# Computing layer 1's modulation vectors piece by piece during layer 0's expert stage

## The chip, the cores and the metric

The kernel runs on one core of a Trainium2 chip. The metric is the device time of one execution in microseconds (us); the time given for a kernel is the median of its runs. The core has TensorE (PE, with its weight loads PEld), VectorE (DVE), ScalarE (ACT), GpSimd (POOL), SyncE (SP), which here only issues transfers, and 16 DMA engines.

## What is computed

Two blocks, one after the other, on 256 tokens of 1024 features, each with two layers. Only the first block is touched by the change. Its layer, cut to what matters here:

```python
cond = jax.nn.silu(c)                       # c: (1, 1024)
for l in range(DEPTH):                      # DEPTH = 2
    mod = cond @ ada_w[l] + ada_b[l]        # 1024 x 6144: the modulation
    sh1, sc1, g1, sh2, sc2, g2 = split(mod, 6)
    h = rms_norm(x, norm1_g[l]) * (1.0 + sc1) + sh1
    proj = h @ w_in[l]                      # then three mixers on its parts
    x = x + g1 * (concat(y_ssd, y_moba, y_swa) @ w_out[l])
    h = rms_norm(x, norm2_g[l]) * (1.0 + sc2) + sh2
    x = x + g2 * peer_ffn(h, ...)           # 8 heads x top 16 of 16384 experts
```

The modulation depends on c alone, not on x: that of layer 1 can be computed at any time. The expert stage peer_ffn is done densely: all 16384 experts' pre-activations are computed (first layer, u), multiplied with a gate that is zero for experts not chosen, and multiplied with v (second layer).

## The kernel before

Products are in fp32 split into two halves of type fp32r ("upper" and "lower"). Each weight part of 1 MB (128x2048 f32) is loaded by SyncE into one of four slots raw, ScalarE copies its upper half (upper_part, L1164), and VectorE (L1494) or GpSimd (L622) subtracts to get the lower half (lower_part). TensorE makes three passes: upper by lower, upper by upper, lower by upper (by_feature L685 and L691, by token L715 and L722, second_layer L920). A slot of raw is free for part n once the lower half of part n - 4 is made; ScalarE and VectorE prepare part n + 2 in turn n (SPLIT = 2).

**The modulation** is the first thing of a layer: twelve tiles of 1024x512 (2 MB, in_ada_w). VectorE sums chunks 0 to 5 of a tile by scalar_tensor_tensor (L1555, L1558), TensorE does chunks 6 and 7 (L760), the bias (L765), and sums VectorE's part over the partitions with a matrix of ones (L767); ScalarE writes the result, the same in all partitions, to mod (L1147). The tiles' slots are the memory in which the weight parts also lie, so in layer 1 the loads start when layer 0's last parts are used up. Between tiles 3 and 4 VectorE norms x and, in both layers, the memory tokens mem, whose transposed form goes out to DRAM.

**The expert stage** of a layer has 128 turns n, in the order of expert_order(): 40 first_layer parts, then two first_layer and two second_layer parts in alternation to turn 87, then 40 second_layer parts. Turns 0 to 19 lie beside the choice of the experts on VectorE; GpSimd makes their lower halves. Turns 20 to 35 also build the gates: for each group of 8 tokens VectorE makes one-hot matrices (hot(i), L1824 and L1825, 16 instructions), TensorE multiplies them (gate_group, L899), ScalarE copies the result to gates_out (L1274), and SyncE writes each pair of groups to DRAM (spill, L565), 1 MB. From there fetch (L574) brings them back by experts. In a loop turn VectorE does, in this order, gate_hidden (where there is one), lower_part(n + 2), and hot for the two groups of the next turn. hot(i) waits for group i - 2. The four zero matmuls that open the accumulators acc (L891) stand before turn 20.

**SyncE's list** in the expert stage is what sets the order of the transfers:

```python
for n, (layer, t, u) in enumerate(expert_order()):
    e = expert_part(l, 0, n)
    sp.wait_ge(*e.raw_free())
    sp.dma_start(raw[:, e.r, :], ...)
    if 0 <= n - 2 * CHOOSE - RAW < GROUPS // 2:      # n = 24 to 39
        spill(n - 2 * CHOOSE - RAW)                  # waits for groups up to 2 (n - 24) + 1
```

Each engine runs a list of its own, in order; a wait holds back all that stands behind it. The first block's two layers are the two turns of a loop (Fori) on each engine.

## Time and profile before

| | us |
|---|---|
| median of 3 runs | 3761.12 |
| lowest and highest | 3759.5, 3761.81 |
| the profiled execution | 3763.92 |
| its span | 3762.1 |
| PE busy | 3430.5 (91%) |
| DVE busy | 2390.1 (64%) |
| ACT busy | 1468.7 (39%) |
| mean DMA | 183 GB/s |

Layer 0 of the first block takes the span from 0 to 1101 us, layer 1 from there to 2193 us, the second block the rest. The busy times are those of the whole span; the stages differ much, so they are read one by one. Busy PE is not PE at its peak. L12 is line 12 of the kernel before.

### The profile page before, as it was taken

The numbers are of one execution on the slowest core, as the hardware profiler recorded it, in microseconds if no ns is written. First come the engines' busy times: TensorE is split into PE (matmuls) and PEld (weight loads), VectorE is DVE, ScalarE is ACT, GpSimd is POOL, SyncE is SP. The second block draws the span as 40 slices with busy tenths as digits, with TensorE's granted clock in tenths as the row PEclk, the third lists the DMA queues.
The fourth block names the chain that finished last, engine by engine and source line by source line (L and its number), as shares of the span: only waits on it lengthen the run. The fifth ranks groups of instructions, "written<-read, shape, count | busy, mean of one in ns | idle before, by whom it ended". The sixth has DMA issues, their size and how long they took to land.

```text
span 3762.1 us, 58692 instructions
## 1 busy us (share of the span) xinstructions
PE 3430.5 (91%) x22220; PEld 3103.9 (83%) x22220; DVE 2390.1 (64%) x4104; ACT 1468.7 (39%) x1545; POOL 229.0 (6%) x48
## 2 busy tenths in 40 slices
PE   6879999999988799999999989996999898968898
PEld 2879899998864789899998889785889797957896
DVE  6657996556777759995557765464545454644454
ACT  1434454333322434444333343443443433434433
POOL 0005600000000008200000000000000000000000
PEclk8989999999998899999999999998999999979999
DMA  8424466667766234466666755450444454513453
GB/s 361 168 77 158 157 224 242 212 210 235 240 254 271 95 126 176 180 233 232 209 215 236 242 215 179 163 195 23 157 148 168 163 180 157 194 53 127 144 180 123
DMA packets 154051, 688.78 MB, mean 183 GB/s; under 512 B 10338, under 2 KB 76770, under 8 KB 78946
## 3 DMA queue, kind: packets, MB, share of 16 engines
q1 hardware_dynamic: 149264, 663.79, 49.6%
q10 hardware_dynamic: 4564, 22.21, 1.6%
q8 instruction: 116, 1.90, 0.2%
q14 instruction: 107, 0.88, 0.1%
HBM read 649.26 MB, written 36.70 MB: 182 GB/s over the span
## 4 chain that ended last, share of the span: by engine, by line
PE 79%; DVE 11%; ACT 3%; issue 2%; DVEq 2%; DMA 1%; PEld 1%; ACTq 0%; PEldq 0%
PE ps L685 25%; PE ps L920 19%; PE ps L691 12%; PE ps L715 9%; PE ps L722 4%; PE ps L899 3%; DMA work<-in_mem 1%; ACT work L1156 1%; PE ps L760 1%; DVE position_hot L1801 1%; PE ps L657 1%; DVE position_hot L1804 1%; DVE scr L1759 1%; DVE scr L1766 1%; PE ps L767 1%
## 5 line engine op out<-in xcount | busy, mean ns | idle before, releaser
L1164 ACT ACTIVATE weights_upper<-weights 128x2048 fp32r<-128x2048 f32 x520 | 995.8, 1916 | 1747.4 <-PE ps L685 972.4
L1494 DVE TENSOR_TENSOR weights_lower<-weights,weights_upper 128x2048 fp32r<-128x2048 f32 x476 | 1089.4, 2289 | 789.9 <-ACT weights_upper L1164 789.1
L685 PE MATMUL ps<-hT_upper,weights_upper 128*128 128x256 f32 x4416 | 626.2, 284 | 3.0 <-ACT hT_upper L1326 2.7
L685 PE MATMUL ps<-hT_lower,weights_upper 128*128 128x256 f32 x4416 | 624.9, 284 | 0.2
L691 PE MATMUL ps<-hT_upper,weights_lower 128*128 128x256 f32 x4416 | 575.3, 283 | 4.2 <-POOL weights_lower L622 4.2
L685 PEld LDWEIGHTS ps<-hT_upper,weights_upper 128*128 128x128 f32 x4416 | 572.0, 192 | 6.4 <-ACT hT_upper L1326 6.3
L685 PEld LDWEIGHTS ps<-hT_lower,weights_upper 128*128 128x128 f32 x4416 | 571.3, 192 | 4.7 <-issue 1.0
L691 PEld LDWEIGHTS ps<-hT_upper,weights_lower 128*128 128x128 f32 x4416 | 549.7, 192 | 5.0 <-POOL weights_lower L622 5.0
L622 POOL TENSOR_TENSOR weights_lower<-weights,weights_upper 128x2048 fp32r<-128x2048 f32 x44 | 228.8, 5213 | 1300.6 <-ACT weights_upper L1164 1300.6
L920 PE MATMUL ps<-weights_upper,hidden_lower 128*128 128x512 f32 x1024 | 253.6, 390 | 0.0
L920 PE MATMUL ps<-weights_lower,hidden_upper 128*128 128x512 f32 x1024 | 252.9, 389 | 0.0
L920 PE MATMUL ps<-weights_upper,hidden_upper 128*128 128x512 f32 x1024 | 252.9, 389 | 0.0
L920 PEld LDWEIGHTS ps<-weights_upper,hidden_upper 128*128 128x128 f32 x1024 | 192.2, 188 | 39.9
L920 PEld LDWEIGHTS ps<-weights_lower,hidden_upper 128*128 128x128 f32 x1024 | 192.2, 188 | 39.9
L920 PEld LDWEIGHTS ps<-weights_upper,hidden_lower 128*128 128x128 f32 x1024 | 190.7, 188 | 38.6
L1825 DVE TENSOR_SCALAR scr<-cst,scr 128x128 f32<-128x128 f32 x512 | 177.2, 346 | 0.0
L1824 DVE TENSOR_SCALAR scr<-cst,scr 128x128 f32<-128x128 f32 x512 | 149.8, 292 | 0.2
L1841 DVE TENSOR_TENSOR hidden_upper<-work,scr 128x512 fp32r<-128x512 f32 x80 | 55.4, 692 | 119.3 <-PE ps L920 119.3
L899 PE MATMUL ps<-scr 128*128 128x128 f32 x1024 | 121.4, 277 | 0.0
L899 PEld LDWEIGHTS ps<-scr 128*128 128x128 f32 x1024 | 119.1, 191 | 0.0
L715 PE MATMUL ps<-weights_upper,ffn_lower 128*128 128x512 f32 x352 | 101.0, 407 | 18.3 <-DVE ffn_lower L1974 18.3
L657 PE MATMUL ps<-diag,x_res 128*128 128x128 f32 x256 | 49.6, 382 | 72.7 <-DVE diag L1905 72.7
(311 smaller groups left out, 3496.6 us busy)
## 6 DMA issues: line engine op xcount, KB each, us to landing
weights<-in_parts SPq DMA_DIRECT2D x264, 1024.0 KB, 4.8
weights<-in_experts SPq DMA_DIRECT2D x256, 1024.0 KB, 4.8
weights<-in_ada_w SPq DMA_DIRECT2D x24, 2048.0 KB, 10.9
scr<-gates SPq DMA_DIRECT2D x32, 1024.0 KB, 8.2
gates<-h SPq DMA_DIRECT2D x16, 1024.0 KB, 4.8
gates<-work SPq DMA_DIRECT2D x16, 1024.0 KB, 4.8
mod<-in_row ACTq DMA_DIRECT2D x3, 1536.0 KB, 6.4
rowp<-in_row ACTq DMA_DIRECT2D x2, 1550.0 KB, 19.7
```

The lines of the kernel that those rows point to most:

```text
L622: g.tensor_tensor(lower[:, p_.r % SPLIT, :], raw[:, p_.r, :], upper[:, p_.r % SPLIT, :].bitcast(F32), ALU.subtract).then_inc(lower_ready, 1)
L657: m = mm(k.bank(name, i)[:, (2 * e + t) * P:(2 * e + t + 1) * P], x[:, t, c * P:(c + 1) * P], diag[:, t, :], start=True, stop=True, skip_g ...
L685: m = mm(bank[:, e * T:(e + 1) * T], up[:, c, e * P:(e + 1) * P], s_[:, c, :], start=(e == 0 and n == 0 and c == 0), stop=False, skip_grou ...
L691: m = mm(bank[:, e * T:(e + 1) * T], lo[:, c, e * P:(e + 1) * P], src[0][:, c, :], start=False, stop=(c == KC - 1), skip_group_check=True)
L715: m = mm(k.bank(name, fill + t)[:, 0:cols], s_[:, c, t * P:(t + 1) * P], up[:, c - 4 * i, 0:cols], start=(n == 0 and c == 0), stop=False, ...
L722: m = mm(k.bank(name, fill + t)[:, 0:cols], src[0][:, c, t * P:(t + 1) * P], lo[:, c - 4 * i, 0:cols], start=False, stop=(c == chunks - 1) ...
L899: m = mm(k.bank("G", j)[:, t * P:(t + 1) * P], hotA[:, i_buf, 4 * j + t, :], hotB[:, i_buf, 4 * j + t, :], start=True, stop=True, skip_gro ...
L920: m = mm(k.bank("acc", 2 * t_ + dh), src[:, u, c, t_ * P:(t_ + 1) * P], w[:, c, dh * NBLK:(dh + 1) * NBLK], start=False, stop=False, skip_ ...
L1164: f(upper[:, p_.r % SPLIT, :], raw[:, p_.r, :], ACT.Copy).then_inc(upper_ready, 1)
L1494: v.tensor_tensor(lower[:, s, :], raw[:, p_.r, :], upper[:, s, :].bitcast(F32), ALU.subtract)\
L1824: v.tensor_scalar(hotA[:, i % 2, j, :], iota, ET[:, 0, t:t + 1], None, ALU.is_equal)
L1825: m = v.tensor_scalar(hotB[:, i % 2, j, :], iota, ET[:, 1, t:t + 1], ET[:, 2, t:t + 1], ALU.is_equal, ALU.mult)
```

## The change

Layer 0's modulation stays as it is. That of layer 1 is computed on VectorE in 24 tiles of 256 columns, each of four pieces (256 rows each, 256 KB): ada_piece(s) adds two chunks of 128 rows, weighted by cond, to an accumulator ada_acc that starts from the bias row. Pieces 0 to 31 are done two a turn in turns 20 to 35, pieces 32 to 95 one a turn in turns 40 to 103 (ada_sub_step). SyncE loads a piece five turns (from turn 40 three turns) further on in its list (load_ada). TensorE sums a finished tile over the partitions with one column of ones, into one row (ada_rows, two turns after the last piece), ScalarE copies the row (ada_take), SyncE writes it to DRAM (keep_row), and ScalarE fetches it back, broadcast to all partitions, into mod (mod_back), in three loads near and after layer 0's end. Layer 1 then starts with a norm like that of h2 (scaled_and_shifted), from sums of squares made by ScalarE. mem is normed and kept in layer 0 only. The loads of the parameters of layer 1 move into layer 0's turns. The zero matmuls for acc now stand behind turn 39. The loops over the first block's layers, and those inside TensorE's expert stage, are written out. The host lays out ada_w[1] in the pieces' order.

```diff
@@ -37,6 +37,10 @@
 GROUPS = T // 8
 CHOOSE = 10
 AHEAD = CHOOSE + GROUPS // 4 + 2
+ADA_COLS = 256
+ADA_TILES = 6 * D // ADA_COLS
+ADA_SUBS = 4 * ADA_TILES
+LACED = GROUPS // 2
 EXPERTS = 4 * TURNS
 EPS1, EPS2 = 1e-5, 1e-6
 
@@ -45,6 +49,7 @@
...
@@ -204,6 +218,12 @@
     return order
 
 
+def ada_sub_step(s):
+
+
+    return 2 * CHOOSE + s // 2 if s < 2 * LACED else 2 * AHEAD + s - 2 * LACED
+
+
 class At:
...
@@ -453,6 +476,14 @@
         hotA = view(scr, 768, 2048, "p (b t i) -> p b t i", b=2, t=8)
         hotB = view(scr, 2816, 2048, "p (b t i) -> p b t i", b=2, t=8)
         gates_out = [view(b, at_, 2048, "p (i t) -> p i t", t=16) for b, at_ in ((h_all, 0), (work, 14336))]
+        ada_acc = [view(scr, 4864 + 256 * j, 256) for j in range(2)]
+        ada_bias_row = view(scr, 5376, 256)
+        ada_row = [scr[0:1, 5632 + 256 * j:5888 + 256 * j] for j in range(2)]
+
+        def ada_sub(s):
+
+            return view(work, (12288 if s < 2 * LACED else 14336) + 512 * (s % 4), 512, "p (c n) -> p c n", c=2)
+
         gates_in = view(scr, 768, 4096, "p (b g i t) -> p b g i t", b=2, g=16, i=8)
...
@@ -575,11 +606,32 @@
                                  gates_dram[:, :, 8 * n:8 * n + 8, :].rearrange("g p i t -> p g (i t)"))\
                         .then_inc(gates_landed[n % 2], 16)
 
+                def load_ada(s):
+
+                    tile = s // 4
+                    if s == 0:
+                        sp.wait_ge(S("chosen"), 1)
+                        sp.wait_ge(S("bias_zero"), 1)
+                        sp.sem_inc(S("held"), 1)
+                    if s % 4 == 0:
+                        if tile:
+                            sp.wait_ge(S("ada_used"), s - 3)
+                        sp.dma_start(ada_bias_row[0:1, :], a["ada_b"][1:2, tile * ADA_COLS:(tile + 1) * ADA_COLS])\
+                            .then_inc(S("ada_bias_in"), 16)
+                    if s >= 4:
+                        sp.wait_ge(S("ada_used"), s - 3)
+                    sp.dma_start(ada_sub(s).rearrange("p c n -> p (c n)"), a["ada_s"][s]).then_inc(ada_landed[s % 4], 16)
+
+                def keep_row(tile):
+
+                    sp.wait_ge(S("ada_taken"), tile + 1)
+                    sp.dma_start(ada_dram[0:1, tile * ADA_COLS:(tile + 1) * ADA_COLS], ada_row[tile % 2])\
+                        .then_inc(ada_kept[tile % 2], 16)
+
                 for n, (layer, t, u) in enumerate(expert_order()):
                     e = expert_part(l, 0, n)
                     sp.wait_ge(*e.raw_free())
-                    sp.dma_start(raw[:, e.r, :], a["experts"][bass.ds(l, 1), n].rearrange("o p n -> p (o n)"))\
-                        .then_inc(raw_landed[e.r], 16)
+                    sp.dma_start(raw[:, e.r, :], a["experts"][l, n]).then_inc(raw_landed[e.r], 16)
                     if 0 <= n - 2 * CHOOSE - RAW < GROUPS // 2:
                         spill(n - 2 * CHOOSE - RAW)
                     if n == 2 * CHOOSE + RAW + GROUPS // 2 + 1:
@@ -587,11 +639,18 @@
                         fetch(1)
                     if layer == 1 and u == 1 and t % 2 == 1 and 2 <= (t + 1) // 2 < TURNS // 2:
                         fetch((t + 1) // 2)
+                    if l + 1 < DEPTH:
+                        for s in range(ADA_SUBS):
+                            if ada_sub_step(s) + (5 if s < 2 * LACED else 3) == n:
+                                load_ada(s)
+                        for tile in range(ADA_TILES):
+                            if ada_sub_step(4 * tile + 3) + 10 == n:
+                                keep_row(tile)
...
-                    by_feature(expert_part(l, it, n), k.bank("U", u), hT1)
-
-                with pe.Fori(0, CHOOSE // 2) as it:
-                    for n in range(4):
-                        first_layer(it, n, it * 2 + n // 2, n % 2)
+                    by_feature(expert_part(l, 0, n), k.bank("U", u), hT1)
+
+                def ada_rows(n):
+
+                    for tile in range(ADA_TILES if l + 1 < DEPTH else 0):
+                        if ada_sub_step(4 * tile + 3) + 2 == n:
+                            name, i = ("early row", tile) if tile < LACED // 2 else ("late row", tile - LACED // 2)
+                            pe.wait_ge(*k.free(name, 0, i))
+                            pe.wait_ge(S("ada_used"), 4 * tile + 4)
+                            mm(k.bank(name)[0:1, 0:ADA_COLS], ones[:, 0:1], ada_acc[tile % 2], start=True, stop=True,
+                               skip_group_check=True).then_inc(k.fill_sem(name), 1)
+
+                order = expert_order()
+                for n in range(2 * CHOOSE):
+                    first_layer(n, *order[n][1:])
 
                 pe.wait_ge(S("chosen"), l + 1)
                 for i in range(2):
...
@@ -886,9 +956,6 @@
                         m = nc.tensor.transpose(k.bank("eT", i)[:, j * P:(j + 1) * P],
                                                 E3[:, 2 * i + j // 2, (j % 2) * P:(j % 2 + 1) * P], ident)
                     m.then_inc(k.fill_sem("eT", i), 1)
-                for i in range(4):
-                    pe.wait_ge(*k.free("acc", i))
...
@@ -896,21 +963,23 @@
                     for j in range(2):
                         pe.wait_ge(*k.free("G", j, i))
                         for t in range(4):
-                            m = mm(k.bank("G", j)[:, t * P:(t + 1) * P], hotA[:, i_buf, 4 * j + t, :],
-                                   hotB[:, i_buf, 4 * j + t, :], start=True, stop=True, skip_group_check=True)
+                            m = mm(k.bank("G", j)[:, t * P:(t + 1) * P], hotA[:, i % 2, 4 * j + t, :],
+                                   hotB[:, i % 2, 4 * j + t, :], start=True, stop=True, skip_group_check=True)
                         m.then_inc(k.fill_sem("G", j), 1)
 
-                with pe.Fori(0, GROUPS // 8) as it:
-                    for n in range(4):
-                        first_layer(it, 2 * CHOOSE + n, it * 2 + (CHOOSE + n // 2), n % 2)
-                        for i_buf in range(2):
-                            gate_group(it * 8 + (2 * n + i_buf))
-                for n in range(2 * CHOOSE + GROUPS // 2, 2 * AHEAD):
-                    first_layer(0, n, n // 2, n % 2)
-
-                def second_layer(it, n, t, u):
-
-                    p_ = expert_part(l, it, n)
+                for n in range(2 * CHOOSE, 2 * AHEAD):
+                    first_layer(n, *order[n][1:])
+                    if n < 2 * CHOOSE + LACED:
+                        for i in range(2):
+                            gate_group(2 * (n - 2 * CHOOSE) + i)
+                    ada_rows(n)
+                for i in range(4):
+                    pe.wait_ge(*k.free("acc", i))
+                    mm(k.bank("acc", i), zeros, cst[:, 0:NBLK], start=True, stop=False, skip_group_check=True)
...
@@ -1275,9 +1362,36 @@
                           k.bank("G", j).rearrange("p (t i) -> p i t", t=4), ACT.Copy)\
                             .then_inc(k.empty_sem("G", j), 1)
 
+                def ada_take(tile):
+
+                    name, i = ("early row", tile) if tile < LACED // 2 else ("late row", tile - LACED // 2)
+                    if tile >= 2:
+                        act.wait_ge(ada_kept[tile % 2], 16 * (tile // 2))
+                    act.wait_ge(*k.filled(name, 0, i))
+                    act.sem_inc(S("held"), 1)
+                    f(ada_row[tile % 2], k.bank(name)[0:1, 0:ADA_COLS], ACT.Copy).then_inc(k.empty_sem(name), 1)
+                    act.wait_ge(*k.emptied(name, 0, i))
+                    act.sem_inc(S("ada_taken"), 1)
+
                 for n, (layer, t, u) in enumerate(expert_order()):
                     if n + SPLIT < EXPERTS:
                         upper_part(expert_part(l, 0, n + SPLIT))
+                    elif l + 1 < DEPTH:
+                        upper_part(part(firsts[l + 1], 0, "win", n + SPLIT - EXPERTS))
+                    if l + 1 < DEPTH:
+                        if n == 2 * CHOOSE + LACED:
+                            act.wait_ge(S("ada_used"), 2 * LACED)
+                        for tile in range(ADA_TILES):
+                            if ada_sub_step(4 * tile + 3) + 3 == n:
+                                ada_take(tile)
+                        if n == 2 * AHEAD + 4 * (TURNS - AHEAD):
+                            mod_back(0, 2)
+                        if n == 112:
+                            act.wait_ge(S("gated"), 2 * (AHEAD + 3))
+                            mod_back(2, 5)
+                        if n == 118:
+                            act.wait_ge(S("gated"), 2 * (AHEAD + 6))
+                            row1_in(1)
                     if layer == 0:
                         gelu(n, t, u)
                     if n == 2 * CHOOSE - 5:
@@ -1288,11 +1402,21 @@
                             gates(2 * (n - 2 * CHOOSE) + i)
                     if n == 2 * AHEAD:
                         act.wait_ge(S("chosen"), l + 1)
-                        act.dma_start(final_g, a["final_g"].rearrange("(o n) -> o n", o=1).broadcast_to([P, D]))\
-                            .then_inc(S("fin_in"), 16)
-                        act.dma_start(colp[:, 0:K2["end"]], a["col2"][0]).then_inc(S("col_in"), 16)
-                act.wait_ge(S("fin_in"), l * 16 + 16)
-                act.wait_ge(S("col_in"), l * 16 + 16)
+                        if l + 1 < DEPTH:
+                            col1_in(1)
+                        else:
+                            act.dma_start(final_g, a["final_g"].rearrange("(o n) -> o n", o=1).broadcast_to([P, D]))\
+                                .then_inc(S("fin_in"), 16)
+                            act.dma_start(colp[:, 0:K2["end"]], a["col2"][0]).then_inc(S("col_in"), 16)
+                if l + 1 < DEPTH:
+                    for t in range(TT):
+                        act.wait_ge(S("x_peer"), l * TT + (t + 1))
+                        square_sum(x[:, t, :], h[:, t, :], t)
+                        deviation(t, t, EPS1_COL)
+                    act.wait_ge(S("first_done"), l + 2)
+                    mod_back(5, 6)
+            act.wait_ge(S("fin_in"), 16)
+            act.wait_ge(S("col_in"), 16)
 
             def rows(l, name, n, signal):
...
+                        v.scalar_tensor_tensor(out=h[:, t, :], in0=x[:, t, :], scalar=RS[:, t:t + 1], in1=gain,
+                                               op0=ALU.mult, op1=ALU.mult)
+                        v.drain()
+                        v.tensor_tensor(h[:, t, :], h[:, t, :], shift, ALU.add).then_inc(S(signal), 1)
+
+                if l == 0:
+                    for i in range(12):
+                        v.wait_ge(*k.emptied("ada", i))
+                    modulated(0, "h1")
+                    for i in (0, 2):
+                        take(k, "mT", i, mem_t[:, 2 * i:2 * i + 2, :])
+                    for n in range(2):
...
@@ -1844,8 +1977,29 @@
                     v.tensor_tensor(hid_lo[:, u, :, :], gact[t % AHEAD][:, u, :, :], hid_up[:, u, :, :].bitcast(F32),
                                     ALU.subtract).then_inc(S("gated"), 1)
 
+                def ada_piece(s):
+
+                    tile = s // 4
+                    acc = ada_acc[tile % 2]
+                    if s % 4 == 0:
+                        if tile >= 2:
+                            j = tile - 2
+                            v.wait_ge(*(k.filled("early row", 0, j) if j < LACED // 2
+                                        else k.filled("late row", 0, j - LACED // 2)))
+                        v.wait_ge(S("ada_bias_in"), 16 * tile + 16)
+                        v.sem_inc(S("held"), 1)
+                    v.wait_ge(ada_landed[s % 4], 16 * (s // 4) + 16)
+                    for c in range(2):
+                        v.drain()
+                        i = 2 * (s % 4) + c
+                        m = v.scalar_tensor_tensor(out=acc, in0=ada_sub(s)[:, c, :], scalar=cT[:, i:i + 1],
+                                                   in1=acc if i else ada_bias_row, op0=ALU.mult, op1=ALU.add)
+                    m.then_inc(S("ada_used"), 1)
+
                 hot(0)
                 hot(1)
+                if l + 1 < DEPTH:
+                    v.memset(ada_bias_row, 0.0).then_inc(S("bias_zero"), 1)
                 v.wait_ge(*expert_part(l, 0, 2 * CHOOSE + SPLIT - 1).lower())
                 for n, (layer, t, u) in enumerate(expert_order()):
                     if n < 2 * CHOOSE:
@@ -1855,13 +2009,27 @@
                         gate_hidden(t + 1, u)
                     if n + SPLIT < EXPERTS:
                         lower_part(expert_part(l, 0, n + SPLIT))
+                    elif l + 1 < DEPTH:
+                        lower_part(part(firsts[l + 1], 0, "win", n + SPLIT - EXPERTS))
                     i = 2 * (n - 2 * CHOOSE) + 2
                     if i < GROUPS:
                         hot(i)
                         hot(i + 1)
+                    if l + 1 < DEPTH:
+                        for s in range(ADA_SUBS):
+                            if ada_sub_step(s) == n:
+                                ada_piece(s)
+                        if n == 122:
+                            v.wait_ge(S("mod_in"), 32)
+                            v.wait_ge(S("par1_in"), 64)
+                            v.sem_inc(S("held"), 1)
+                            v.scalar_tensor_tensor(out=mod[:, D:2 * D], in0=mod[:, D:2 * D], scalar=1.0,
+                                                   in1=rowp[:, R1["n1"]:R1["n1"] + D], op0=ALU.add, op1=ALU.mult)
                     if n == 2 * AHEAD - 3:
                         gate_hidden(0, 0)
                         gate_hidden(0, 1)
+                if l:
+                    v.wait_ge(S("mod_in"), 48)
                 for t in range(TT):
                     for nb in range(2):
...
@@ -1874,9 +2042,9 @@
                 v.drain().then_inc(S("first_done"), 1)
 
 
-            v.wait_ge(S("fin_in"), 16 * DEPTH)
+            v.wait_ge(S("fin_in"), 16)
```

## Rows read from the trace of the kernel before

**Rows 1.** Busy time by stage: window, length, busy us (count) of PE PEld DVE ACT POOL, clock, DMA.
```profile
441.10:596.90 155.80, 155.80 (x1331) 155.80 (x1330) 147.67 (x512) 78.61 (x97) 0.00 (x0) 1.00 0.59 212
596.90:872.40 275.50, 275.50 (x1826) 254.66 (x1825) 157.82 (x121) 107.91 (x77) 0.00 (x0) 1.00 0.65 221
1100.90:1193.60 92.70, 63.36 (x139) 23.35 (x138) 75.23 (x105) 16.88 (x25) 0.00 (x0) 0.83 0.83 338
```

**Rows 2.** Timeline of one turn: start us, us, engine, line, operation.
```profile
512.35 3.79 PE L899 MATMUL ps<-scr 128*128 128x128 f32 x32
...
513.29 2.30 DVE L1494 TENSOR_TENSOR weights_lower<-weights,weights_upper 128x2048 fp32r<-128x2048 f32 x1
...
515.50 0.29 DVE L1824 TENSOR_SCALAR scr<-cst,scr 128x128 f32<-128x128 f32 x1
...
516.19 0.60 ACT L1274 ACTIVATE work<-ps 128x512 f32<-128x512 f32 x1 [0.30 <-PE ps L899]
...
516.87 0.33 SPq L565 DMA_DIRECT2D gates<-work  x1
...
517.49 0.33 SPq L581 DMA_DIRECT2D weights<-in_experts  x1
...
522.74 2.29 DVE L1494 TENSOR_TENSOR weights_lower<-weights,weights_upper 128x2048 fp32r<-128x2048 f32 x1
```

**Rows 3.** Timeline of the stage's first two turns.
```profile
447.05 2.29 DVE L1494 TENSOR_TENSOR weights_lower<-weights,weights_upper 128x2048 fp32r<-128x2048 f32 x1 [2.35 <-ACT weights_upper L1164]
...
456.51 2.28 DVE L1494 TENSOR_TENSOR weights_lower<-weights,weights_upper 128x2048 fp32r<-128x2048 f32 x1
...
460.59 0.33 SPq L565 DMA_DIRECT2D gates<-work  x1
```

**Rows 4.** Waits of SyncE's queue: in total us, times, longest.
```profile
SPq L564 <- ACT h L1274: 147.9, 16, 17.6
```

**Rows 5.** Timelines of three hand-overs: behind the experts, before h2T, before yT.
```profile
1101.02 1.29 DVE L1869 TENSOR_TENSOR scr<-ps,mod 128x512 f32<-128x512 f32 x2 [6.73 <-PE ps L941]
...
1199.68 0.87 PEld L715 LDWEIGHTS ps<-weights_upper,hT_upper 128*128 128x128 f32 x4
...
1312.37 3.27 PEld L641 LDWEIGHTS ps<-cst,h 128*128 128x128 f32 x16 [10.31 <-issue]
...
1321.58 0.87 PEld L715 LDWEIGHTS ps<-weights_upper,hT_upper 128*128 128x128 f32 x4
...
1341.99 0.16 DVE L1735 RECIPROCAL stats<-stats 128x1 f32<-128x1 f32 x1 [0.99 <-ACT stats L1142]
...
1346.32 1.23 DVE L1740 TENSOR_TENSOR h<-h,mod 128x1024 f32<-128x1024 f32 x1
...
2193.29 1.29 DVE L1869 TENSOR_TENSOR scr<-ps,mod 128x512 f32<-128x512 f32 x2 [6.73 <-PE ps L941]
...
2198.45 0.29 ACT L1142 ACTIVATE stats<-stats 128x1 f32<-128x1 f32 x1
```

**Rows 6.** One line's instructions: durations ns min/median/max, first and last start, forms.
```profile
L1712 DVE SCALAR_TENSOR_TENSOR h<-h,stats,rowp x12: 479/480/752, 216.8 to 1311.6; 128x256 f32<-128x256 f32 x8, 128x512 f32<-128x512 f32 x4
```

**Rows 7.** Groups by line, 1100.9 to 1194: busy, mean ns, idle time before.
```profile
L1558 DVE SCALAR_TENSOR_TENSOR mod<-weights,stats,mod 128x512 f32<-128x512 f32 x60 | 45.1, 751 | 4.5
```

**Rows 8.** Chain of work, in layer 1's modulation: start us, us, what.
```profile
1119.51 3.34 PE ps L760 x4
...
1125.21 1.95 PE ps L760 x4
```

**Rows 9.** DMA issues between 430 and 600 us: KB each, us to landing.
```profile
weights<-in_experts SPq DMA_DIRECT2D x18, 1024.0 KB, 6.7
gates<-h SPq DMA_DIRECT2D x8, 1024.0 KB, 4.8
```

**Rows 10.** Landing of the loads of line 1293 (colp, 164 KB).
```profile
DMA to landing us min/median/max: 3.6/3.9/4.1
```

**Rows 11.** Timeline of a turn with second_layer alone.
```profile
1090.02 0.69 DVE L1841 TENSOR_TENSOR hidden_upper<-work,scr 128x512 fp32r<-128x512 f32 x1 [1.09 <-PE ps L920]
```

238 lines of the change are left out of this document (129 added, 109 removed).

## The prediction

> **What bounds the kernel now.** I read the table of busy time by stages first, because the change touches one stretch of layer 0 and the stretch behind it. In layer 0's gate stage (441 to 597 us) and behind it TensorE is busy all the time at the full clock; between 1101 and 1194 us, where layer 1's modulation is computed, it is busy 63 of 93 us, VectorE 75, and the DMA engines 83% [rows 1]. So a transfer and a sum of 93 us lie bare between two expert-bound stretches, and what is worth asking is what the 16 turns before them can carry. A "turn" is one n of expert_order(); turns 20 to 35 of layer 0 each hold one first_layer part and two gate groups.
>
> The second view is the timeline of one such turn [rows 2]. TensorE's two gate groups take 3.8 us of it, the expert part the rest. VectorE repeats after 9.45 us (522.74 - 513.29): lower_part 2.2 us, then two hot() of 3.63 us each (7.26 us, from 515.50 to the next lower_part). It has no idle time in between, so the stage runs on two engines at once: whatever is added to VectorE here is added to the span. Over the whole stage VectorE waits once, 2.35 us before its first lower_part [rows 3].
>
> The third view is SyncE, which issues the transfers in program order. Its spill of a pair of gate groups waits for ScalarE's last copy of these groups; where that copy went to h, 16 such waits make 147.9 us [rows 4], and there are as many for the copies that go to work. In turn 21 the spill goes out at 460.59, while VectorE was done with the hot() of these groups before 456.51 [rows 3]. SyncE is thus paced by the gate groups, one spill per turn.
>
> **What the change removes, step by step.** From the first DVE instruction behind the expert sum (L1869, 1101.02) to the second win part (1199.68) before: 98.7 us [rows 5]. After: x of the first token tile, Square, table load and Sqrt take 5.45 us (2193.29 to 2198.45 + 0.29, the same chain before the final norm); from there two reciprocals, scalings and additions of 128x1024 take 5.56 us (1341.99 to 1346.32 + 1.23) and 0.1 of hand-over; then the second half of 16 transposes, upper and lower halves and the first part of a by-token product take 7.6 us (1314.0, the middle of the transposes that start at 1312.37, to 1321.58) [rows 5]. Sum 18.8 us, so 79.9 us are removed. Layer 1's twelve loads of 2 MB, their matmuls, the second norm of mem and its write all go with it; SyncE, ScalarE and VectorE have two win parts ready before, since these ride in the last two turns. ScalarE's Exp for a_log with its table load comes while VectorE makes h1, and is hidden.
>
> **What it adds in turns 20 to 35.** Each turn gets two pieces (ada_piece), each two scalar_tensor_tensor of 128x256 with a drain. One of 128x256 takes 0.48 us, one of 128x512 0.75 [rows 6]; a drain puts 0.07 between two of them (4.5 us of idle time for 60) [rows 7]. Four make 2.2 us, with the waits 2.3.
>
> The larger term is when their data comes. load_ada(s) stands in SyncE's list at n = turn + 5, behind spill(n - 24) of the same n, that is spill(turn - 19). This spill needs gate group 2(turn - 19) + 1 copied out; TensorE makes that group in turn + 1, from the hot() that VectorE does last in this same turn, right before it waits for the piece. So VectorE asks for data whose load is issued only after its own last result has gone through TensorE, ScalarE, the spill and the queue. The wait can't be worked off in advance; it comes in every turn. Its length from the end of hot():
> - TensorE's group: 1.9 us at full speed (half of 3.79), start and hand-over 0.1; ScalarE's last copy 0.6 and 0.1 of hand-over, so the spill goes out 2.7 us after hot() (from rows 2: matmuls end 516.14, copy 516.19 to 516.79, spill 516.87). TensorE will have stood idle some 8 us before it. Behind the pauses of the modulation stretch its matmuls ran at 1.2 GHz: 3.34 us for four against 1.95 at 2.4 GHz [rows 8]; the first of the two groups would take about 3.7 us and part of the second too. All of the last group slow would be 4.6 us, none 2.7; I take 3.7, half of it slow, since in rows 8 the full clock was back 5.7 us after a slow stretch had begun, which is about where the last group is half done.
> - the landing: a spill of 1 MB lands after 4.8 us. An expert part of 1 MB issued 0.6 us behind a spill lands after 6.7, not 4.8 [rows 9]. With S for the spill's issue that is S + 7.3, which is the spill's 4.8 and 2.5 for its own 1 MB. A piece is a quarter of that, so the first lands at S + 5.4, the second at S + 6.1. Issue (0.62 apart [rows 2]) is in time for that. Were small loads to pass the spill, the nearest row is colp's load, behind one of final_g, which lands after 3.6 to 4.1 [rows 10]: S + 0.6 + 3.6 = S + 4.2 at the least.
> - the two pieces, 2.3 us, the second of which has landed by then.
>
> So 3.7 + 5.4 + 2.3 = 11.4 us a turn. The last hot() is in turn 34, so 14 turns (20 to 33) delay it: 160 us. Ends: 2.7 + 4.2 + 2.3 = 9.2, or 129 us; 4.6 + 5.4 + 2.3 and 1.1 more if each 128x256 took what 128x512 took (0.75), 13.4, or 188 us.
>
> The Trainium skill, "TensorE: Matmul & The Clock Gate", section "HAM oscillation — how this bites in real kernels", says that a loop whose matmul bursts are separated by waits for DMA starts every burst at the low clock again. The trace agrees for a single pause (3.34 against 1.95 us); that it recurs each turn nothing in it shows. By the rule the last group is late by 1.0 us a turn, without it the sum would be 14 us lower. The skill's "DMA: Bandwidth & Descriptors", section "Anatomy of one DMA — SWDGE (gpsimd) path", puts the fixed cost of a transfer at about 2 us; a piece that met no queue would land about 2.6 us after its issue, an estimate by that page, and the sum would be 14 x 2.2 = 31 us lower. The 6.7 us speak against it.
>
> Before turn 20: the four zero matmuls for acc (L891) leave the place ahead of the gate stage. first_layer(20) starts that much earlier, its upper half ends earlier, and with it VectorE's only wait (2.35) goes, for the most part: -2.3 us (at the other end nothing). At the end, the last group is done 3.0 us behind its hot(), now 2.4 (worked out as for rows 2: one turn of TensorE's stands 0.5 us behind VectorE's): +0.6.
>
> **What it adds behind turn 35.** The last pieces hold lower_part(37), and ScalarE waits for ada_used 32 before gelu(36), on which TensorE's bank for turn 38 hangs: worked through, turn 38 starts 1.6 us late. The four zero matmuls are now between busy turns: two matmuls of 512 columns, four records, take 1.95 at full speed [rows 8], so four take 3.9 us. Row sums: 24 matmuls with 256 columns, half of 0.98, with hand-over 0.55; the first eight lie in time in which TensorE waits, 16 add 8.8 us. (Nothing to 0.98 each: 0 to 16.) Pieces at one a turn in turns 40 to 103: VectorE has much room to turn 87 (158 of 275 us busy) [rows 1], and from 88 to 103 it idles about 1.09 us a turn [rows 11] against 1.15 for a piece: 1 us. Their loads stand three turns ahead and behind no spill, so they are there. Queue order: ahead of each load SyncE waits for ada_used s - 3, long given; keep_row at +10 meets a row taken at +3. On ScalarE the row copy stands behind the same turn's upper_part and ahead of gelu; it costs 0.3 to 0.6 us there, and the cover is U's other bank: nothing on the path, 0.6 a row (14 us) if that cover were gone. row1_in in turn 118 has to land by turn 122, some 22 us on; it is 1.5 MB, and 1 MB behind 1 MB landed after 6.7 [rows 9]: nothing, with 4 us as the other end. The fetches of mod (turns 88 and 112) have still more time. Sum: 1.6 + 3.9 + 8.8 + 1 = 15.3.
>
> Layer 1 has no pieces; its zero matmuls move too (+3.9), and its gate stage, begun sooner, ends up to 2.8 us earlier, from where VectorE bounds it: +1.1. Unrolling: TensorE shows no gap at the ends of its inner loops (155.80 busy of 155.80, 275.50 of 275.50) [rows 1], so nothing.
>
> **Sum.** -2.3 + 160 + 0.6 + 15.3 - 79.9 + 1.1 = +94.8 us. The profiled execution took 3763.9 (span 3762.1), 2.8 above the median; I add the sum to the median: 3856.
>
> **The rivals.**
> A. The pieces' data is there in time, and only the arithmetic counts (the wait for the spill is not where I put it). Then 14 x 2.3 = 32.2, less 2.3 at the start and 0.9 of slack (hot() ends before its group starts): +29.0, then 3.9 + 8.8 + 1 without the jam at turn 36, - 79.9 + 1.1, in all -36: 3725, faster. Against it speaks SyncE's order with its waits [rows 4]. Were even this work hidden, it would be some 30 us less still; with VectorE never idle in the stage that is all but excluded. Break-even is at a turn's cost of some 4.6 us.
> B. Pieces pass the spill on the DMA engines. 14 x (3.7 + 4.2 + 2.3) = 143: 3839. For it: they use other buffers and are small; against it the 6.7 us.
> C. TensorE is at the low clock through the whole last group and the pieces are dearer than their size, 188 us for 160: 3884.
> D. The change doing less than it says: layer 1's modulation still on the path at the end. The last row is kept by turn 113 of 128 and what is fetched after the layer is a block that is first used at layer 1's end; nothing speaks for it.
>
> **How the numbers follow.** Forecast 0.74, B 0.11, C 0.08, A 0.06, near no change by a mix 0.01. Range 3820 to 3888: it holds the forecast with its spread, B and C. A measurement can tell about 0.2% from no change. Faster 0.06, same 0.01, slower 0.93.
>
> **What would show it.** The gate stage of layer 0, from 441 to 597 now, lasts about 310 us; a turn repeats after about 21 us; VectorE waits in each for a DMA that writes work from in_ada_s, about 9 us; the piece's load is issued right behind a spill; TensorE is busy about half, its mean granted clock near 0.75. From L1869 to the second win part some 19 us. Wrong would be: VectorE without idle time in the stage (A), landings under 4 us (B), or a stage after turn 40 that grows by more than 20 us.

## The result, and the profile after

The changed kernel takes 3853.36 us (median of four runs, 3852.62 to 3858.38) against 3761.46 before: a ratio of 1.0243, with a 95% interval from 1.023 to 1.0256. It is slower by 92 us; 3856 was predicted, a rise of 95. The profiled execution took 3858.38, the highest of its four; its span is 3856.1, 94.0 more than that of before.

| | before | after |
|---|---|---|
| span of the profiled execution | 3762.1 | 3856.1 |
| PE busy | 3430.5 (91%) | 3424.5 (89%) |
| DVE busy | 2390.1 (64%) | 2425.2 (63%) |
| layer 0's end (closing matmul L941, now L1006) | 1100.7 | 1275.1 |
| layer 1's end (the same matmul) | 2193.0 | 2291.8 |

The same table of busy time by stage as [rows 1], of the kernel after. The columns are window, length, busy us (count) of PE, PEld, DVE, ACT and POOL, granted clock, DMA share and GB/s:

```profile
441.10:750.00 308.90, 189.02 (x1298) 180.02 (x1297) 175.70 (x582) 79.91 (x102) 0.00 (x0) 0.77 0.36 129
773.00:1100.00 327.00, 327.00 (x1964) 286.70 (x1963) 241.40 (x261) 124.89 (x95) 0.00 (x0) 1.00 0.74 257
```

The gate stage, full on two engines before, now lasts about 309 us, and neither TensorE nor VectorE is busy for more than 62% of it. Behind it TensorE is full again. Which wait it is can be read from the waits between 430 and 1260 us (total us, times, longest):

```profile
DVE scr L1995 <- DMA work<-in_ada_s: 133.9, 19, 9.1
...
PE ps L966 <- DVE scr L1958: 119.8, 15, 9.5
...
SPq L595 <- ACT h L1361: 135.3, 8, 18.0
SPq L595 <- ACT work L1361: 129.6, 8, 17.9
```

VectorE waits for the pieces' transfer, TensorE for VectorE's hot(), and SyncE stands at the spill's wait for the copies of the gates (L595), up to 18.0 us at a time. One turn from the timeline, to be laid beside [rows 2]:

```profile
577.53 5.67 PE L966 MATMUL ps<-scr 128*128 128x128 f32 x32 [9.47 <-DVE scr L1958]
...
580.74 0.35 DVE L1958 TENSOR_SCALAR scr<-cst,scr 128x128 f32<-128x128 f32 x1
...
583.23 0.60 ACT L1361 ACTIVATE work<-ps 128x512 f32<-128x512 f32 x1 [0.24 <-PE ps L966]
...
583.90 0.33 SPq L596 DMA_DIRECT2D gates<-work  x1
...
584.60 1.59 SPq L623 DMA_DIRECT2D work<-in_ada_s  x2
...
589.41 2.18 DVE L1995 SCALAR_TENSOR_TENSOR scr<-work,stats,scr 128x256 f32<-128x256 f32 x4 [8.33 <-DMA work<-in_ada_s]
...
591.51 2.29 DVE L1618 TENSOR_TENSOR weights_lower<-weights,weights_upper 128x2048 fp32r<-128x2048 f32 x1
```

This is the ring of the prediction: hot() ends at 581.09, its groups' last copy at 583.83, the spill goes at 583.90, the pieces' transfers behind it, and VectorE resumes at 589.41. The same ring is in the chain that ended last, at the first such turn (start, us, what):

```profile
457.55 2.07 PE ps L966 x16
459.64 0.61 ACT work L1361
460.32 0.33 SPq L596
460.78 0.30 SPq L619
461.13 4.50 DMA work<-in_ada_s
```

And it repeats, by the first and the last of 15 spills:

```profile
460.32 0.33 SPq L596 DMA_DIRECT2D gates<-work  x1
...
747.35 0.33 SPq L596 DMA_DIRECT2D gates<-work  x1
```

(747.35 - 460.32) / 14 = 20.50 us a turn. Before it was 9.45 by VectorE's turns, as in the prediction: 11.05 more, 154.7 in all, where 11.4 and 160 were predicted. By the spills it was 9.38 before (460.59 to 591.91), which would make 155.7, so the total is good to about 1 us. The transfers of the stage (size of each, median us from issue to landing):

```profile
weights<-in_experts SPq DMA_DIRECT2D x17, 1024.0 KB, 6.9
...
gates<-work SPq DMA_DIRECT2D x8, 1024.0 KB, 4.8
work<-in_ada_s SPq DMA_DIRECT2D x32, 256.0 KB, 5.1
```

The hand-over from layer 0 to layer 1, where before the 98.7 us of [rows 5] were:

```profile
1275.11 0.95 PE L1006 MATMUL ps<-cst 128*128 128x2 f32 x8
1275.49 2.29 DVE L1618 TENSOR_TENSOR weights_lower<-weights,weights_upper 128x2048 fp32r<-128x2048 f32 x1 [3.15 <-ACT weights_upper L1229]
1277.70 1.28 DVE L2037 TENSOR_TENSOR scr<-ps,mod 128x512 f32<-128x512 f32 x2
...
1283.17 0.16 DVE L1691 RECIPROCAL stats<-stats 128x1 f32<-128x1 f32 x1 [0.35 <-ACT stats L1207]
...
1287.50 1.23 DVE L1696 TENSOR_TENSOR h<-h,mod 128x1024 f32<-128x1024 f32 x1
...
1290.47 2.06 PE L774 MATMUL ps<-weights_upper,hT_upper 128*128 128x512 f32 x4
...
1297.67 0.87 PEld L774 LDWEIGHTS ps<-weights_upper,hT_upper 128*128 128x128 f32 x4
```

From the expert sum (L2037) to the second win part it is 20.0 us, 18.8 predicted. From TensorE's last matmul it is 22.6, where it was 99.0 (1100.70 to 1199.68).

**Where the 94.0 us are.** Up to layer 0's last matmul +174.4, from there through layer 1 -75.6, the second block -4.8. Of the first, 3.1 stand ahead of the gate stage (VectorE's L1813 at 429.15 is now L1946 at 432.24). How far such differences can be trusted, stretches with the same code show. In the nine traces of the changed kernel and of the versions below, VectorE reaches this instruction between 427.4 and 432.4 us, and the second block takes 1562.7 to 1570.8 us; in the eight of them with the same layer 1 that layer takes 1012.8 to 1020.9 us. A difference of some 5 us between two traces in one stretch is thus no evidence for the edit, and the 3.1 and the 4.8 are of that size.

### The profile page after: what moved, and what is told of

Same layout as the page of the kernel before. It is cut to its first block, busy times and chain, and to the rows that moved or that the text cites. A ratio compares the mean times of both kernels' runs of the same rounds, so it can differ in the third digit from the quotient of the medians.

```text
span 3856.1 us, 56123 instructions
## 1 busy us (share of the span) xinstructions
PE 3424.5 (89%) x22156; PEld 3119.2 (81%) x22156; DVE 2425.2 (63%) x4210; ACT 1476.7 (38%) x1559; POOL 229.4 (6%) x48
## 4 chain that ended last, share of the span: by engine, by line
PE 74%; DVE 14%; ACT 3%; DMA 3%; issue 2%; DVEq 1%; PEld 1%; ACTq 0%; SPq 0%; PEldq 0%
PE ps L744 22%; PE ps L989 18%; PE ps L750 11%; PE ps L774 9%; PE ps L781 4%; PE ps L966 4%; DMA work<-in_ada_s 2%; DVE weights_lower L1618 1%; ACT work L1221 1%; DMA work<-in_mem 1%; DVE scr L1958 1%; DVE scr L1957 1%; DVE position_hot L1934 1%; PE ps L716 1%; DVE position_hot L1937 1%
## 5 line engine op out<-in xcount | busy, mean ns | idle before, releaser
L966 PE MATMUL ps<-scr 128*128 128x128 f32 x1024 | 155.0, 318 | 121.4 <-DVE scr L1958 121.4
L966 PEld LDWEIGHTS ps<-scr 128*128 128x128 f32 x1024 | 146.8, 228 | 128.5 <-DVE scr L1958 125.0
L1995 DVE SCALAR_TENSOR_TENSOR scr<-work,stats,scr 128x256 f32<-128x256 f32 x192 | 93.1, 485 | 148.5 <-DMA work<-in_ada_s 133.9
L1958 DVE TENSOR_SCALAR scr<-cst,scr 128x128 f32<-128x128 f32 x512 | 182.7, 357 | 0.0
L1957 DVE TENSOR_SCALAR scr<-cst,scr 128x128 f32<-128x128 f32 x512 | 155.9, 304 | 0.2
```

Of the source, the lines that this page charges most:

```text
L966: m = mm(k.bank("G", j)[:, t * P:(t + 1) * P], hotA[:, i % 2, 4 * j + t, :], hotB[:, i % 2, 4 * j + t, :], start=True, stop=True, skip_gro ...
L1957: v.tensor_scalar(hotA[:, i % 2, j, :], iota, ET[:, 0, t:t + 1], None, ALU.is_equal)
L1958: m = v.tensor_scalar(hotB[:, i % 2, j, :], iota, ET[:, 1, t:t + 1], ET[:, 2, t:t + 1], ALU.is_equal, ALU.mult)
L1995: m = v.scalar_tensor_tensor(out=acc, in0=ada_sub(s)[:, c, :], scalar=cT[:, i:i + 1], in1=acc if i else ada_bias_row, op0=ALU.mult, op1=AL ...
```

## The experiments

The theory: the ring through the spill sets each of the 14 turns, and the arithmetic of the two pieces is a fifth of their price. Rivals: the arithmetic itself, beside an already full VectorE; the size of the transfer ahead in the queue; TensorE's low clock.

**The pieces' transfers ahead of the spill.** The same work; only SyncE's order changes:

```diff
                     sp.dma_start(raw[:, e.r, :], a["experts"][l, n]).then_inc(raw_landed[e.r], 16)
+                    if l + 1 < DEPTH:
+                        for s in range(ADA_SUBS):
+                            if ada_sub_step(s) + (5 if s < 2 * LACED else 3) == n:
+                                load_ada(s)
                     if 0 <= n - 2 * CHOOSE - RAW < GROUPS // 2:
                         spill(n - 2 * CHOOSE - RAW)
...
-                        for s in range(ADA_SUBS):
-                            if ada_sub_step(s) + (5 if s < 2 * LACED else 3) == n:
-                                load_ada(s)
```

> SyncE's load of a piece stands ahead of the spill of the same n instead of behind it; all else is as in the changed kernel (3853). My theory: each of turns 20 to 33 costs 11.05 us more than before (a spill every 20.50 us against 9.45), of which only 2.2 are arithmetic; the rest is the wait for a load issued behind a spill that hangs on VectorE's own last hot(). With the load one turn earlier the wait goes: a turn of about 11.7 us, 14 x 8.8 = 123 us less, about 3730, VectorE without a DMA wait in the stage. Rival (DMA latency and queue, not the order): the queue is as full, the wait moves and most of the 9 us stay, 3830 to 3855. Rival (arithmetic and turnaround of VectorE): no change, 3853.

Measured: 3733.62 us, 0.9927 of before (0.991 to 0.9944), 120 us below the changed kernel. Its spills repeat after 12.02 us (455.77 to 624.06), and VectorE's wait for the pieces has shrunk from 133.9 us to

```profile
DVE scr L1996 <- DMA work<-in_ada_s: 11.2, 6, 6.1
```

A turn is 2.57 us longer than before, and two pieces are 2.2 to 2.3 of that; in ten of the 14 turns VectorE repeats after 11.7 us, which is the pieces alone. So the arithmetic of rival A was priced rightly; the rest of a turn, 20.50 - 12.02 = 8.5 us, is the order of two lines in SyncE's list. The transfers land later here (6.7 us, behind an expert part), and it costs nothing, since they are asked for a turn ahead. The Trainium skill, "DMA: Bandwidth & Descriptors", section "Anatomy of one DMA — SWDGE (gpsimd) path", says that a semaphore wait for a DMA happens on the sequencer that issues it, before dispatch, and not on the DMA engines. The trace agrees: what held the pieces was SyncE standing at L595 for up to 18.0 us, while the engines were at 36%.

**The transfers behind the spill's wait, but ahead of its 1 MB.** This parts the wait from the queue:

```diff
                     for j in range(2):
                         sp.wait_ge(*k.emptied("G", j, 2 * n + 1))
+                    for s in first:
+                        load_ada(s)
                     sp.dma_start(gates_dram[n], gates_out[n % 2]).then_inc(gates_spilled[n % 2], 16)
```

> SyncE still waits for the gate groups before it loads a piece, but issues the piece's transfer ahead of the spill's 1 MB and not behind it. My theory: the dependency stays, the queueing behind 1 MB goes; a piece then lands some 3.2 us after its issue and not 5.1, and the issue of the first comes 0.4 us sooner: 14 x 2.3 = 32 us less, 3821. Rival (small transfers pass the large one anyway, or each costs a fixed 5 us): no change beyond 14 x 0.4 = 6 us, 3847.

Measured: 3819.28 us (3816.34 to 3823.53), 34 less than the changed kernel. 17.76 us a turn, and the landing, median of the stage:

```profile
work<-in_ada_s SPq DMA_DIRECT2D x32, 256.0 KB, 3.0
```

So of the 8.5 us a turn 2.7 (20.50 - 17.76) are the place behind the spill: 2.1 in the landing, behind its megabyte in the queue, and about 0.6 in the issue, which in the changed kernel comes 0.4 to 0.7 us behind the spill's. The other 5.7 are the wait with the bare transfer. This also decides rival B of the prediction, under which pieces pass the spill: they don't, 5.1 us behind it against 3.0 ahead of it. The Trainium skill's same page, section "Queues, rings and completion order", says that an engine's descriptors are consumed in ring order; the trace agrees. Its fit with a fixed cost of about 2 us is given for transfers issued by GpSimd; the estimate of 2.6 that the prediction worked out from it for an unqueued piece is 0.4 under the 3.0 measured here for SyncE. In the changed kernel the pieces stood behind the spill, with 5.1.

**Filler for TensorE's clock.** Seven products of zeros with 512 columns in each of turns 21 to 35:

```diff
+                    if l == 0 and n == 2 * CHOOSE + 1:
+                        pe.wait_ge(*k.free("acc", 3))
+                    if l == 0 and 2 * CHOOSE < n < 2 * CHOOSE + LACED:
+                        for _ in range(7):
+                            mm(k.bank("acc", 3), zeros, cst[:, 0:NBLK], start=True, stop=True, skip_group_check=True)
```

> The changed kernel (3853), with seven matmuls of zeros, 128x512, after each first_layer of turns 21 to 35 of layer 0, into a bank of the accumulators that is opened anew later; about 6.9 us of the 8 in which TensorE waits for hot(). They keep its clock at 2.4 GHz. The prediction's term, with the Trainium skill's rule on waits: half of the last group slow, 1.0 us a turn, so 14 us less, 3839. My theory now, from the trace of after: the slow matmuls are those of the first group, which end before VectorE's second hot() does; the spill goes out 2.9 us after hot() and not 3.7, so filling gives 0 to 2 us, 3852, though the granted clock of the stage rises from 0.77 to nearly 1.

Measured: 3859.83 us (3856.33 to 3861.04), no gain, 6 us more if anything. Busy time and clock of the two kernels between 460 and 740 us, first the changed kernel, then the one with the filler:

```profile
460.00:740.00 280.00, 162.40 (x1097) 154.51 (x1095) 155.09 (x500) 68.05 (x87) 0.00 (x0) 0.76 0.37 132
```

```profile
460.00:740.00 280.00, 237.51 (x1302) 179.29 (x1301) 155.22 (x501) 68.88 (x88) 0.00 (x0) 0.94 0.36 132
```

The clock rose from 0.76 to 0.94, and the mean turn stayed at 20.51 us. That mean hides two things that cancel. In ten of the 14 turns the filler did its work. Both gate groups run at the full clock, 2.05 us each:

```profile
578.45 2.05 PE L966 MATMUL ps<-scr 128*128 128x128 f32 x16 [2.65 <-DVE scr L1963]
582.07 2.05 PE L966 MATMUL ps<-scr 128*128 128x128 f32 x16 [1.56 <-DVE scr L1963]
```

In these ten the spill goes out 2.8 to 3.0 us behind the end of hot(), 2.83 in the mean, and VectorE repeats after 20.1 us. In the other four the clock had fallen all the same (0.57 between 515.1 and 523.0 us), and the last group is slow:

```profile
515.12 2.99 PE L966 MATMUL ps<-scr 128*128 128x128 f32 x16 [1.85 <-DVE scr L1963]
518.75 3.78 PE L966 MATMUL ps<-scr 128*128 128x128 f32 x16 [0.63 <-DVE scr L1963]
...
523.24 0.33 SPq L596 DMA_DIRECT2D gates<-h  x1
```

Here hot() ends at 518.69, and the spill goes 4.55 us behind it (3.9 to 4.6 in the four): the 4.6 that the prediction gave for a last group that is all slow. So the low clock is on the path where it reaches the last group. In the changed kernel it covers the first group and the start of the last. Both together take 5.67 us in the turn above (577.53), 1.6 more than at full speed, but at the end of the second hot(), 581.09, only 2.1 us are left, so that turn loses next to nothing. In others more of the last group is slow; the spill goes 2.8 to 3.4 us behind hot(), 3.14 in the mean of the 14. The low clock thus costs the changed kernel 3.14 - 2.83 = 0.3 us a turn, some 4 us in all. The Trainium skill's rule ("TensorE: Matmul & The Clock Gate", section "HAM oscillation — how this bites in real kernels") holds, a burst behind each wait starts slow, but of the 14 us that the prediction worked out by it only these 4 are there.

About as large as the 6 us more is what the first filled turn lost: there the filler held TensorE until 456.7, 4 us behind the end of hot(), and the first two spills are 15.1 us apart (446.24, 461.38) where they were 9.3.

**Half of the arithmetic.** Each early piece adds one of its two chunks; the other half of the sum of the first eight tiles is left out:

```diff
-                    for c in range(2):
+                    for c in range(1 if s < 2 * LACED else 2):
```

> Pieces 0 to 31 add one chunk of 128 rows and not two (half of the sum of the first eight tiles is left out); loads and waits as in the changed kernel. My theory: wait and arithmetic are in series in every turn, so two instructions of 0.55 us each less per turn give 14 x 1.1 = 15 us less: 3838. Rival (the load bounds the turn and arithmetic is hidden behind it): no change, 3853. For a turn that were bound by VectorE's total work alone it would be 15 too, so what tells is that the DMA wait stays at about 134 us in total.

Measured: 3851.09 us (3844.45 to 3855.24), 2 us less than the changed kernel, where 15 were expected. With runs that spread over 11 us the times decide nothing. Its profiled execution, the fastest of the four, has 19.65 us a turn, 0.85 less. VectorE's waits:

```profile
DVE scr L1995 <- DMA work<-in_ada_s: 139.7, 30, 9.5
```

There are 30 waits where there were 19, since VectorE now mostly waits for the second piece too; but these second waits are short (0.17 us at 599.80). From the spill to the end of the pieces a turn takes 6.75 us in the mean where it took 7.83: the expected 1.1 went, in full. What came back is between hot() and the spill, 3.38 us for 3.14, because the low clock reaches further into the last group. In one such turn hot() ends at 688.22, and both groups take 6.8 us, where they took 5.67 in the turn shown above:

```profile
684.66 6.83 PE L966 MATMUL ps<-scr 128*128 128x128 f32 x32 [7.68 <-DVE scr L1958]
...
692.20 0.33 SPq L596 DMA_DIRECT2D gates<-work  x1
```

The arithmetic is in series with the wait, as expected; that the rest of the ring would stay as it was, the expectation took for granted.

**All pieces behind turn 40**, two a turn to turn 71 and one from there on, all loads three turns ahead, all row sums in the later bank, and ScalarE's wait at turn 36 left out:

```diff
-    return 2 * CHOOSE + s // 2 if s < 2 * LACED else 2 * AHEAD + s - 2 * LACED
+    return 2 * AHEAD + s // 2 if s < 64 else 2 * AHEAD + s - 32
```

> No piece in turns 20 to 35: pieces 0 to 63 go two a turn to turns 40 to 71, 64 to 95 one a turn to 72 to 103, all loads three turns ahead; all 24 rows in the bank of the late ones. My theory: the gate stage returns to its 9.45 us a turn (155 us less), the jam of 1.6 us behind it goes, and eight rows more fall on busy TensorE (0.5 us each, +4): about 3700, that is 61 us below the kernel before, if VectorE's idle time in turns 40 to 71 (117 of 275 us were idle to turn 87) carries two pieces a turn of 2.2 us. Rival (that stage has no room after all, since VectorE's idle time lies in places where it waits for ScalarE): 10 to 30 us of it come back as TensorE idle, 3710 to 3730. Rival (loads of the pieces crowd out the parts): TensorE waits for upper halves of weights, over 3730.

Measured: 3703.15 us (3702.4 to 3707.15), 0.9848 of before (0.9832 to 0.9864), the fastest version: it beats both kernels. The gate stage is nearly as it was before, 9.52 us a turn by its spills (460.47 to 593.78) for 9.38, and TensorE is full in it:

```profile
460.00:600.00 140.00, 139.77 (x1178) 138.23 (x1178) 133.12 (x463) 70.83 (x87) 0.00 (x0) 1.00 0.63 225
```

Among VectorE's waits there is none for the pieces. Layer 0 ends 22.8 us later than before (1123.52 against 1100.70), of which 24 row sums at 0.52 and the zero matmuls at 3.6 make 16.1, and 3.3 stand ahead of the gate stage (432.4 for 429.1); I haven't taken the other 3.4 apart. Layer 1 with its hand-over is 79.5 shorter, the second block 4.8: 3762.1 + 22.8 - 79.5 - 4.8 = 3700.6, its span (3700.7).

The last three are edits of this fastest version, each for one small term.

**Row sums over 2 columns** in place of 256, which leaves out layer 1's modulation but for two columns of each tile:

```diff
-                            mm(k.bank(name)[0:1, 0:ADA_COLS], ones[:, 0:1], ada_acc[tile % 2], start=True, stop=True,
+                            mm(k.bank(name)[0:1, 0:2], ones[:, 0:1], ada_acc[tile % 2][:, 0:2], start=True, stop=True,
```

> The kernel with all pieces late (3703), the 24 row sums over 2 columns and not 256 (the modulation of layer 1 is left out but for 2 columns of each tile). Theory: each of 24 rows holds TensorE 0.52 us by the trace and would hold it about 0.1: 24 x 0.42 = 10 us less, 3693. Rival (the rows lie in gaps, TensorE is held by VectorE there): no change.

Measured: 3697.59 us (3694.15 to 3700.94), 5.6 less. In the two traces one record (two a row sum), at 256 columns and at 2:

```profile
L943 PE MATMUL ps<-scr,cst x48: 377/378/378, 641.9 to 1003.4; 128*1 128x256 f32 x48
```

```profile
L943 PE MATMUL ps<-scr,cst x48: 164/164/166, 638.9 to 991.1; 128*1 128x2 f32 x48
```

By the records 48 x 0.213 = 10.2 us should have gone. The times, which spread over 7 us, show about half. The stretch that holds the row sums shows nearly all of it: from VectorE's instruction ahead of the gate stage (L1942) to layer 0's last matmul it is 691.1 us in the fastest version (432.4 to 1123.5) and 681.5 here (429.5 to 1111.0), 9.6 less. The remainder is in layer 1, 8 us longer here with the same code, within the spread given above. The term (8.8 for 16 row sums) thus has the right size.

**The last lower half behind the update of x**, so that it isn't ahead of the expert sum in VectorE's list:

```diff
-                    elif l + 1 < DEPTH:
-                        lower_part(part(firsts[l + 1], 0, "win", n + SPLIT - EXPERTS))
+                    elif l + 1 < DEPTH and n + SPLIT == EXPERTS:
+                        lower_part(part(firsts[l + 1], 0, "win", 0))
...
                 v.drain().then_inc(S("first_done"), 1)
+                if l + 1 < DEPTH:
+                    lower_part(part(firsts[l + 1], 0, "win", 1))
```

> The kernel with all pieces late (3703), VectorE's lower_part of the second win part moved behind the update of x at layer 0's end. Theory: in the trace of after this lower_part (2.3 us) stands ahead of the first multiplication behind the experts, which starts 1.6 us later than TensorE lets it; moving it gives 1.6 to 2 us, 3701. It is needed again only after the first win part, some 10 us on, so nothing comes back. Rival: it then delays the lower half of hT, nothing is gained.

Measured: 3703.06 us (3701.74 to 3704.86), no difference. The expert sum is no longer late (0.31 us behind TensorE's last matmul, 2.59 in the fastest version), but the moved instruction now stands ahead of the reciprocal:

```profile
1120.73 1.29 DVE L2032 TENSOR_TENSOR scr<-ps,mod 128x512 f32<-128x512 f32 x2 [3.08 <-PE ps L1004]
...
1126.06 2.29 DVE L1614 TENSOR_TENSOR weights_lower<-weights,weights_upper 128x2048 fp32r<-128x2048 f32 x1 [0.20 <-issue]
1128.27 0.16 DVE L1687 RECIPROCAL stats<-stats 128x1 f32<-128x1 f32 x1
```

From the expert sum to the reciprocal it is now 7.5 us for 5.5, so that 2.1 of the 2.3 us come back. Nothing is gained, as the rival had it, though what the instruction delays is the reciprocal and not the lower half of hT.

**The zero matmuls back ahead of the gate stage:**

```diff
+                for i in range(4):
+                    pe.wait_ge(*k.free("acc", i))
+                    mm(k.bank("acc", i), zeros, cst[:, 0:NBLK], start=True, stop=False, skip_group_check=True)
+
                 def gate_group(i):
```

> The kernel with all pieces late (3703), the four zero matmuls that open the accumulators back ahead of the gate stage, in both layers. My terms: behind turn 39 they cost 3.9 us, ahead of turn 20 they delay VectorE's stage by 2.3 to 2.8: putting them back gives 1.1 to 1.6 us a layer, 3700. Rival (ahead of the stage they are hidden in full): 8 less, 3695. Rival (they cost their slow 5.9 us there): 4 more, 3707.

Measured: 3708.57 us (3698.26 to 3711.37). The runs spread over 13 us, so it can't be told from no change, nor from the rival's 3707. A term of 3 to 5 us can't be settled by the times of this kernel. In the traces the stretch from L1942 to layer 0's last matmul takes 691.3 us (427.8 to 1119.1), for 691.1 without the edit: in layer 0 the place of the zero matmuls makes no difference that one trace of each can show.

## Why the prediction was right, and where its steps were off

- **The ring** was found in SyncE's list ahead of the result, and it is what happened; with the loads ahead of the spill it is gone. It costs 11.05 us a turn; 11.4 were predicted.
- **Two of its terms were off in opposite directions.** From the end of hot() to the spill I took 3.7 us, half of the last group slow. It is 2.8 in the turn shown (581.09 to 583.90), one of the shortest, 3.4 in the longest and 3.14 in the mean of the 14: less of the last group is slow than I took. From the spill to the end of the pieces I took 5.4 + 2.3 = 7.7. It is 7.6 in the turn above (583.90 to 591.51), 8.6 in two turns where the second piece lands late and VectorE waits a second time, as at 570.61, where that wait is 0.89 us, and 7.83 in the mean. The first term alone would have made the sum 14 x 0.56 = 8 us too high; with the second it is 5.3 too high.
- **The start of the stage:** -2.3 predicted. VectorE's first lower half there starts at 448.0, 1.0 later than before, behind a stretch that is 3.1 later: -2.1.
- **Behind turn 35:** 15.3 and 0.6 for the last group were predicted, 15.9. What is left of layer 0 (174.4 - 3.1 + 2.1 - 154.7) is 18.7. The zero matmuls took 3.60 for 3.9. The waits at turn 36 are in the trace (ScalarE 7.28 us for ada_used); what they cost the path was not measured by itself.
- **The hand-over:** 79.9 predicted, 76.4 measured (99.0 less 22.6). Two steps were short. VectorE's list has a lower half of 2.29 us right ahead of the expert sum, which I had only counted as done before: the sum starts 2.59 us behind TensorE's end, 0.32 before. And the first matmuls on h1 run slowly behind the pause (four records in 2.06 us, later 1.07): 8.9 for the 7.6 of the last step.
- **Layer 1** apart from the hand-over: +0.8, predicted +1.1. With a spread of 8 us in this layer between traces the agreement is luck.
- **The second block is 4.8 us shorter**, which nothing in the prediction has. Two other versions (pieces ahead of the spill and all late) have 4.8 too, but all nine traces lie between 1562.7 and 1570.8 us, and the 1569.1 of before lies among them, so it isn't shown that the change did it. One thing differs in a visible way. Before, VectorE stood between two instructions on the path to TensorE's transposes, waiting for nothing the profile shows:

```profile
2979.51 0.16 DVE L1899 RECIPROCAL stats<-stats 128x1 f32<-128x1 f32 x1 [3.30 <-issue]
2982.67 0.28 DVE L1905 TENSOR_SCALAR diag<-cst,stats 128x128 f32<-128x128 f32 x1 [2.99 <-issue]
```

After, and in seven of the eight other versions, such a stop comes three instructions later, ahead of a lower half that is not needed yet:

```profile
3079.90 0.16 DVE L2067 RECIPROCAL stats<-stats 128x1 f32<-128x1 f32 x1 [3.22 <-issue]
3080.14 0.29 DVE L2073 TENSOR_SCALAR diag<-cst,stats 128x128 f32<-128x128 f32 x1
...
3083.43 2.29 DVE L1618 TENSOR_TENSOR weights_lower<-weights,weights_upper 128x2048 fp32r<-128x2048 f32 x1 [2.56 <-issue]
```

What stops the engine there was not tried. The 3.1 us ahead of the gate stage stay open too.

The sum of 94.8 thus meets the 94.0 of the spans through errors that cancel: -5.3 in the ring, +2.8 behind turn 35, +3.1 ahead of the gate stage, +3.5 at the hand-over, -0.1 in the start and in layer 1, -4.8 in the second block. That it comes so close is in part luck. The median is another 2 us lower, mostly because the profiled execution of after lies 5.0 above its median and that of before 2.8 above the median to which the sum was added. The range would have needed only some 10 us to either side for what really varied; most of its width was for the rivals B and C, and neither of their conditions holds in the changed kernel: pieces don't pass the spill (5.1 us for 3.0), and the last group is never slow throughout (3.4 us at most for 4.6).

## What to carry to other kernels

Before a load is put into an issuing engine's list, look at the wait ahead of it there, and ask whether what that wait is for hangs on the engine that will use the load: if it does, each turn pays the whole way round, and prefetching five turns ahead in program order doesn't help. Moving the issue ahead of the wait turned +92 us into -28 here. And work that is cheap but not free goes where its engine has idle time (turns 40 to 103), not into a stage that its engine fills already: that was another 30 us.

## What was not expected of the hardware

- A slow clock costs only where it reaches the last work ahead of the next hand-over. With a mean clock of 0.76 over 280 us the changed kernel lost some 0.3 us a turn by it. In the four turns of the filler version in which it covered the last group, the spill went out up to 1.7 us later (4.55 behind hot() for 2.83), though the mean clock there was 0.94.
- 256 KB behind 1 MB in the same queue landed after 5.1 us, ahead of it after 3.0; and the megabyte behind them then took 5.9 instead of 4.8.
- A stop of VectorE of 2 to 3 us that no wait explains stands at another instruction in the changed kernel than before, three further on. What causes it is open.
- The same code took 5 to 8 us more or less from one trace to another, in each of three stretches. Each version has one trace, so it isn't known whether the version or the single execution makes the difference; either way, differences of this size aren't evidence for an edit.
